# Expert token lists scattered to memory in the router, and experts run by falling count in three size classes

## The reference, cut to what matters

```
scores = sigmoid(x @ w_router)                      # (1088, 64)
biased = scores + router_bias
# 8 groups of 8 experts; the best 4 groups by the sum of their two best stay
_, idx = top_k(where(group_kept, biased, -inf), 8)  # 8 experts for each token
sel = take_along_axis(scores, idx, axis=1)
wts = sel / sum(sel) * 2.5
for e in range(64):
    tok = tokens with e in idx
    y[tok] += wts * ((silu(x[tok] @ w_gate[e]) * (x[tok] @ w_up[e])) @ w_down[e])
out = y + shared_expert(x)
```

## Time and profile before

| | |
|---|---|
| median of three runs | 2150.04 us (2149.35 to 2150.91) |
| span of the profiled execution | 2147.0 us |
| PE busy | 1883.8 us, 88% |
| PE weight loads busy | 1525.1 us, 71% |
| DVE busy | 1348.0 us, 63% |
| ACT busy | 868.2 us, 40% |
| POOL busy | 400.5 us, 19% |
| mean granted clock of TensorE | 0.928 |
| read from HBM, written | 330.71 MB, 66.34 MB |

### The profile page before, as it was taken

How to read it: one execution, slowest core, us unless ns; L and a number is a source line. 1 busy time by engine, 2 the same in 40 slices (tenths; PEclk the granted TensorE clock), 3 DMA queues, 4 the chain that set the end, 5 groups by cost and what they waited for, 6 DMA issues and landing times. The chain is left out here.

```text
span 2147.0 us, 35537 instructions
## 1 busy us (share of the span) xinstructions
PE 1883.8 (88%) x12638; PEld 1525.1 (71%) x12639; DVE 1348.0 (63%) x2002; ACT 868.2 (40%) x1392; POOL 400.5 (19%) x367
## 2 busy tenths in 40 slices
PE   7999999789968998899999989989989898747887
PEld 4566665457757897888888878888888798633433
DVE  3333433269856786767777777767666677556774
ACT  2122222133224555455555545555545555431111
POOL 0100001000011111211111121121111112135662
PEclk9999999889979998999999999999989899878999
DMA  9000000210066776767777777777676687655652
GB/s 358 35 0 0 0 0 13 85 52 29 30 208 221 255 267 219 258 225 252 263 251 246 258 244 248 251 258 264 227 254 235 226 277 247 214 203 179 229 199 103
DMA packets 104971, 396.27 MB, mean 185 GB/s; under 512 B 13230, under 2 KB 26990, under 8 KB 87901
## 3 DMA queue, kind: packets, MB, share of 16 engines
q1 hardware_dynamic: 61877, 245.27, 34.3%
q0 software_dynamic: 27264, 95.08, 13.0%
q10 hardware_dynamic: 15808, 55.65, 6.4%
HBM read 330.71 MB, written 66.34 MB: 185 GB/s over the span
## 5 line engine op out<-in xcount | busy, mean ns | idle before, releaser
L1352 POOL DMA_INDIRECT rows<-rows_dram,idx x132 | 228.2, 1728 | 1085.0 <-issue 1085.0
L1364 PE MATMUL GU<-x_hi,hi_g 128*128 128x212 f32 x1024 | 283.2, 277 | 0.0
L1364 PE MATMUL GU<-x_hi,hi_u 128*128 128x212 f32 x1024 | 282.7, 276 | 0.0
L1364 PE MATMUL GU<-x_lo,hi_g 128*128 128x212 f32 x1024 | 281.6, 275 | 0.0
L1364 PE MATMUL GU<-x_hi,lo_g 128*128 128x212 f32 x1024 | 281.2, 275 | 0.0
L1364 PE MATMUL GU<-x_lo,hi_u 128*128 128x212 f32 x1024 | 280.7, 274 | 0.0
L1364 PE MATMUL GU<-x_hi,lo_u 128*128 128x212 f32 x1024 | 280.3, 274 | 0.0
L1387 PE MATMUL T<-ident,rows 128*128 128x128 f32 (+1 forms) x1040 | 149.3, 314 | 137.9 <-DMA rows<-rows_dram,idx 137.9
L1522 DVE TENSOR_TENSOR x_lo<-T,x_hi 128x424 fp32r<-128x424 f32 x260 | 145.5, 595 | 144.8 <-ACT x_hi L1447 135.8
L1387 PEld LDWEIGHTS T<-ident,rows 128*128 128x128 f32 (+1 forms) x1040 | 132.9, 178 | 140.9 <-issue 140.9
L183 DVE TENSOR_TENSOR lo_u<-raw_u,hi_u 128x2048 fp32r<-128x2048 f32 x65 | 149.0, 2293 | 124.8 <-ACT hi_u L176 124.8
(11 more groups left out here) (240 smaller groups left out, 3481.0 us busy)
## 6 DMA issues: line engine op xcount, KB each, us to landing
raw_g<-in_w_exp_gate SPq DMA_DIRECT2D x65, 1024.0 KB, 7.0
raw_u<-in_w_exp_up SPq DMA_DIRECT2D x65, 1024.0 KB
raw_d<-in_w_exp_down SPq DMA_DIRECT2D x65, 1024.0 KB, 7.7
y_dram<-y ACTq DMA_DIRECT2D x64, 512.0 KB
y_dram<-y ACTq DMA_DIRECT2D x64, 336.0 KB
rows_dram<-row SPq DMA_DIRECT2D x9, 512.0 KB, 2.7
w_big<-in_w_in SPq DMA_DIRECT2D x2, 2048.0 KB, 12.4
w_out<-in_w_out SPq DMA_DIRECT2D x1, 4096.0 KB, 18.1
```

What stands on the lines that cost most here:

```text
L1352: pool.indirect_dma_start(out=rows[0:BLK[b], b, :], out_offset=None, in_=rows_dram[:, :], in_offset=bass.IndirectOffsetOnAxis(ap=idx[0:BLK ...
L1364: ins = pe.matmul(out, lhs[x], rhs[w], start=first and i == 0, stop=last and i == 2)
```

## The change

1. **Lists in memory.** `list_dram` holds for each place in a list and each expert a pair (token, row for an overflow). It is filled with a spare value in the mixer, by one transfer from a constant. In the router VectorE computes for each pair an `entry` = place x 64 + expert, and GpSimd scatters eight transfers of 128 values of 8 bytes for each tile (`enter`). After the last tile SP loads the first 256 places of all lists into `lists`.
2. **Ranks.** After the last tile two small matmuls and some ten VectorE operations rank the experts by count (expert 0 is always first, since its weights are loaded already), give `order`, and for each expert the first row of its results and its cap (`base_dram`).
3. **Three classes.** The expert stage runs the experts by rank: 16 with 212 rows, 16 with 164 (128 + 36), 32 with 128. Each class is a loop and, written out behind it, its last expert, which prepares one of the next class's size. All tiles of tokens, hidden layer and rows are cut to the class's size. Where an expert has more tokens than its cap, a general loop (`each_extra`) runs over all 64 experts with 128 rows; for none it does nothing.
4. **No list work in the expert stage.** `make_list`, `to_index` and `one_hot` are gone. GpSimd copies the index out of `lists` and gathers as soon as the transposes of the expert before are done. With each of the first nine experts GpSimd also gathers, in eight transfers of 8-byte values, the bases of one tile's pairs (`find_rows`); VectorE makes `slots` from them after the 16th expert.
5. The 65th expert is not prepared. Stores of the two blocks have a semaphore each.

```diff
...
-CAP = 212
-ROUNDS = -(-(SEQ + NS) // CAP)
-BLK = (P, CAP - P)
-OVER_ROW = E * CAP
-SPARE_ROW = OVER_ROW + (SEQ + NS) * TOP
-Y_ROWS = SPARE_ROW + CAP
+SIZES = ((212, 16), (164, 16), (128, 32))
+CAP = SIZES[0][0]
+RANK_CAP = [cap for cap, n in SIZES for _ in range(n)]
+RANK_ROW = [sum(RANK_CAP[:r]) for r in range(E)]
+TWO_BLOCKS = sum(n for cap, n in SIZES if cap > P)
...
+            sp.dma_start(list_dram[0:LIST_ROWS * E].rearrange("(p n) a -> p (n a)", p=LIST_ROWS), c["list0"]).then_inc(
+                keep["list_set"], 16)
...
+            sp.wait_ge(keep["listed"], 16 * TILES * TOP)
+            sp.dma_start(keep["lists"][:], list_dram[0:2 * P * E].rearrange("(b p e) a -> p b e a", b=2, e=E)).then_inc(
+                list_ld, 16)
+            sp.wait_ge(list_ld, 96)
+            sp.wait_ge(based, 1)
+            sp.dma_start(base_dram[:, :], base_i[:]).then_inc(base_st, 16)
+            sp.wait_ge(base_st, 16)
...
+            def enter(t):
+                pool_after(pool, keep["passed"], entry_ready, t + 1)
+                for k in range(TOP):
+                    pool.indirect_dma_start(
+                        out=list_dram[:, :], out_offset=bass.IndirectOffsetOnAxis(
+                            ap=entry[:, t, k:k + 1] if isinstance(t, int) else
+                            entry[:, bass.ds(t, 1), k:k + 1].rearrange("p a k -> p (a k)"), axis=0),
+                        in_=value[:, t, k, :], in_offset=None).then_inc(keep["listed"], 16)
...
+            norm(1)
+            pool.wait_ge(list_ld, 16 * 5)
+            pool.wait_ge(keep["list_set"], 16)
+            for t in range(TILES):
+                if t + 2 < TILES:
+                    norm(t + 2)
+                enter(t)
...
             def places(t):
                 dve.wait_ge(count_done, t + 1)
-                own.did(dve.scalar_tensor_tensor(out=pe_pos[:], in0=C[:, 0:E], scalar=1.0, in1=maskf[:],
-                                                 op0=ALU.add, op1=ALU.mult))
-                own.wait()
-                own.did(dve.tensor_copy(place[:, 0:E, t], pe_pos[:]))
+                own.did(dve.tensor_tensor(pe_pos[:], C[:, 0:E], maskf[:], ALU.mult))
                 own.did(dve.tensor_tensor(sofar[:], sofar[:], maskf[:], ALU.add))
+                own.wait()
+                dve.tensor_copy(sums[:, 0:1], sums[:, 1:2]).then_inc(placed, 1)
                 hot_sum(pe_pos[:], pos8[:, t, :])
-                own.wait()
-                dve.tensor_copy(sums[:, 0:1], sums[:, 1:2]).then_inc(placed, 1)
+                pos = pos8[:, t, :]
+                if isinstance(t, int) and t == LAST:
+                    own.did(dve.tensor_tensor(spared[:], pos, spare, ALU.add))
+                    own.wait()
+                    pos = spared[:]
+                own.did(dve.tensor_copy(keep["chosen"][:, bass.ds(t * TOP, TOP)], i8[:]))
+                dve.scalar_tensor_tensor(out=entry[:, t, :], in0=pos, scalar=float(E), in1=idx8[:, t, :],
+                                         op0=ALU.mult, op1=ALU.add).then_inc(entry_ready, 1)
...
+            own.did(dve.scalar_tensor_tensor(out=key[:], in0=C[0:E, 0:E], scalar=float(E), in1=tie[0:E, 0:E],
+                                             op0=ALU.mult, op1=ALU.add))
...
+            dve.tensor_scalar(at_rank[:], iota_e[0:E, :], rank[:], None, ALU.is_equal).then_inc(ranks_ready, 1)
...
+def each_job(eng, body, skip=0):
+    first = 0
+    for i, (cap, n) in enumerate(SIZES):
+        following = SIZES[i + 1][0] if i + 1 < len(SIZES) else None
+        with eng.Fori(max(first, skip), first + n - 1) as job:
+            body(job, cap, cap)
+        body(first + n - 1, cap, following)
+        first += n
+def each_extra(eng, keep, body):
+    n = eng.value_load(keep["extra"][0:1, 0:1], min_val=0, max_val=EXTRA)
+    with eng.Fori(0, n) as r:
+        with eng.Fori(0, E) as rank:
+            body(r, rank, E + r * E + rank)
+def blocks(cap):
+    return [(b, min(P, cap - b * P)) for b in range(-(-cap // P))]
...
+            sp.wait_ge(rows_ld[0], 16)
+            with sp.Fori(0, E - 1) as n:
+                e = sp.value_load(order[0:1, bass.ds(n + 1, 1)], min_val=0, max_val=E - 1)
+                at = sp.snap(n * GATE_PIECE)
+                load(e, n + 1)
...
+            def gather(tokens, cap):
+                for b, n in blocks(cap):
+                    pool.indirect_dma_start(
+                        out=rows[0:n, b, :], out_offset=None, in_=rows_dram[:, :],
+                        in_offset=bass.IndirectOffsetOnAxis(ap=tokens[0:n, b:b + 1], axis=0),
+                    ).then_inc(rows_ld[b], 16)
+            def fetch(job, cap):
+                e = pool.value_load(order[0:1, bass.ds(job, 1)], min_val=0, max_val=E - 1)
+                pool_after(pool, keep["passed"], x_tr, 4 * job + 1)
+                n = len(blocks(cap))
+                pool.tensor_copy(idx[:, 0:n], lists[:, 0:n, bass.ds(e, 1), 0].rearrange("p b e -> p (b e)")).then_inc(
+                    idx_ready, 1)
+                pool_after(pool, keep["passed"], idx_ready, job + 1)
+                gather(idx, cap)
+            fetch(0, CAP)
+            def find_rows(t):
+                for k in range(TOP):
+                    at = t * TOP + k
+                    pool.indirect_dma_start(
+                        out=keep["based"][:, at, :], out_offset=None, in_=base_dram[:, :],
+                        in_offset=bass.IndirectOffsetOnAxis(ap=keep["chosen"][:, at:at + 1], axis=0)).then_inc(base_ld, 16)
+            def job(n, cap, following):
+                if following:
+                    fetch(n + 1, following)
+            for n in range(TILES):
+                fetch(n + 1, CAP)
+                find_rows(n)
+            each_job(pool, job, TILES)
...
-            def make_list(j, h, rows_read):
-                pe.wait_ge(hot_ready, h + 1)
-                pe.wait_ge(idx_ready, j + 1)
-                pe.wait_ge(x_lo_ev, rows_read)
-                for b in range(2):
-                    for t in range(TILES):
-                        ins = pe.matmul(L[:, 2 * b:2 * b + 2], hot[:, t, b * P:(b + 1) * P], tok[:, t, :],
-                                        start=(t == 0), stop=(t == TILES - 1))
-                ins.then_inc(l_done, 1)
...
+            def transposes(m, cap):
+                pe.wait_ge(rows_ld[0], 16 * m + 16)
+                if cap > P:
+                    pe.wait_ge(rows_ld[1], 16 * m + 16)
...
+            def gate_up(m, cap):
+                pe.wait_ge(x_lo_ev, 4 * m + 5)
+                for mat, off in (("g", 0), ("u", cap)):
                     pe.wait_ge(lo_set[mat], m + 1)
                     for f in range(FC):
                         for k in range(KC):
                             w = slice(f * P, (f + 1) * P)
-                            ins = three(GU[f][:, off:off + CAP], (hi[mat][:, k, w], lo[mat][:, k, w]),
-                                        (x_hi[:, k, :], x_lo[:, k, :]), k == 0, k == KC - 1)
+                            ins = three(GU[f][:, off:off + cap], (hi[mat][:, k, w], lo[mat][:, k, w]),
+                                        (x_hi[:, k, 0:cap], x_lo[:, k, 0:cap]), k == 0, k == KC - 1)
...
+            def job(n, cap, following):
+                gate_up(n, cap)
+                if following:
+                    transposes(n + 1, following)
+                down(n, cap)
+            each_job(pe, job)
...
+            def job(n, cap, following):
+                rank = RANK_CAP.index(cap)
+                first = (n - rank) * cap + RANK_ROW[rank]
+                first = first if isinstance(n, int) else act.snap(first)
+                act.activation(warm[:], warm[:], ACT.Sigmoid).then_inc(warmed, 1)
+                if following:
+                    act.wait_ge(ld["g"], 16 * n + 32)
+                    act.wait_ge(g_used, n + 1)
+                    split_hi(act, keep, "g", n + 1, 0)
+                sigmoids(n, cap)
+                if following:
+                    x_parts(n + 1, following)
+                    act.wait_ge(ld["u"], 16 * n + 32)
+                    split_hi(act, keep, "u", n + 1, 0)
+                for b, rows_b in blocks(cap):
+                    if not (isinstance(n, int) and n == 0):
+                        act.wait_ge(y_st[b], 16 * n + 1)
+                    copy_out(n, cap, b, rows_b, 0)
+                    if b == 0 and following:
+                        split_hi(act, keep, "u", n + 1, 1)
+                    copy_out(n, cap, b, rows_b, 1)
+                    store(first, n, b, rows_b)
+                if following:
+                    act.wait_ge(ld["d"], 16 * n + 32)
+                    split_hi(act, keep, "d", n + 1, 0)
...
+            def rows_of_tokens():
+                row, is_over, shift = (slot_f[:, i, :] for i in range(3))
+                dve.wait_ge(base_ld, 16 * TILES * TOP)
+                own.did(dve.tensor_tensor(row, keep["based"][:, :, 0], keep["pos8"][:], ALU.add))
...
+            def job(n, cap, following):
```

(82 more changed lines are left out.)

460 lines of the change are left out of this document (166 added, 294 removed).

## The result

The changed kernel takes 5213.0 us at the median of four runs (5208.6 to 5228.1), the kernel before 2149.7 (2145.8 to 2150.9). The ratio is 2.426, 95% interval 2.421 to 2.431. The forecast was 1903, faster.

A forecast was written before the change was run, and what follows sets the result against it. TensorE was taken as the bound, losing 205.8 us to late gathers and half clock. Terms -258.7 (stage), +3.6 (router), +13 and +2 (handover), -6.8 (end) sum to -246.9: span 1900.1, run 1903; range 1870 to 1975.

The forecast's parts named there:

- An overflow pass, slower than before: Rival, expert stage: one expert over its cap sends all 64 through the general loop, at least 1366 us, 3270; 2%.
- my bound: General loop in an overflow: at least 64 x (14.45 + 6.9 for the splits) us, weights not loaded ahead.
- Down matmuls stay as they are: Expert stage: down matmuls unchanged by the size classes, since one-block experts skipped the second block already.
- In the 164 class they shrink to 36 columns, 0.3: Expert stage: second-block transposes in the 164-row class narrow, saving 0.3 us an expert, giving 17.5.
- My price of a transpose: Expert stage: a transpose of 84 columns costs 0.073 us, from the 1.48 us that 16 take.
- the first step: Expert stage: earlier gathers remove the 34 waits and the half clock behind them; gain 205.8 us, less 2.2.
- 2 for the clock: Router to first expert: 2 us more for a clock that has been low for longer.
- Columns count: Rival, expert stage: gate-up matmuls with fewer columns take less time, 103 us more gain, 1800; 5%.
- GpSimd is the bound: Rival: GpSimd limits router (9 x 2) and first experts (9 x 3.5) where it got work; +50, 1953; 17%.
- The weight chain: Rival, last class: weight loading at 265 GB/s bounds an expert at 16.1 us; +52, 1955; 17%.
- 3.6 + 13: Delay of the first gate-up: router +3.6 us for VectorE's entries, handover to the first expert +13.

The follow-up runs named there:

- e1_guard: Changed kernel with the loop over overflow passes put in If(n > 0) on all engines: 2115.4 us, ratio 0.980 to the kernel before.
- e2_guard_ahead: e1_guard with semaphore y_ev starting at 2, as in the kernel before, not 1, and two waits moved by 1: 1962.9 us, ratio 0.913.
- e11_in_pairs: e2_guard_ahead with each expert's 16 transposes reordered, two of 128 partitions then two of 36, instead of one and one: 1923.9 us, ratio 0.897.
- e12_in_eights: e11_in_pairs with all eight transposes of 128 partitions first, then the eight of 36: 1914.7 us, ratio 0.893.
- e4_two_classes: e2_guard_ahead without the 164-row class, 32 experts of 212 rows and 32 of 128: 1908.1 us, ratio 0.888.
- e8_base_first: e4_two_classes with SyncE storing the experts' first rows ahead of its wait for the scatters: 1905.8 us, ratio 0.886.

## Why the prediction was wrong, point by point

**The step that failed in kind: "An overflow pass, slower than before".** The mechanism was among the rivals with 2%, but I let it hang on the 33rd count and argued that nothing overflows. Nothing does. I never asked what the loop does when its count is 0; `Fori` with an end held in a register does not skip. The kernel before has the same loop over rounds, where the count is at least 1, so no row of it could show this. It costs 3064 us in the changed kernel's profile (the output stage starts at 4993 instead of 1924.2 + 4.6). Its size was off as well: at least 21.35 us an expert by my bound, 48 measured, as scatter, list, gather and transposes stand in one chain and TensorE falls to half clock. With 2% on it, 5213 lay outside the range, and beyond that rival's own 3270.

**"Down matmuls stay as they are".** They don't: the deletion of one `sem_inc` makes each half wait for the one before. e1_guard to e2_guard_ahead: 152.5 us by the medians, 156.2 by the two profiled executions. These 156.2 are 43 in the first class (20.68 against 17.80 an expert), 86 in the middle one, whose clock gains too, and (15.57 - 14.62) x 32 = 30 in the last, less 3.4 by which the first gate-up is later. How much of the 86 is waits and how much clock is not told apart. I compared waits line by line but not the starting values of the semaphores; the deleted line is in the change.

**"In the 164 class they shrink to 36 columns, 0.3".** The sign was wrong: transposes of 36 rows between ones of 128 cost 2.0 us more an expert, and clock behind that. Worth 54.8 us. My price of a transpose was a mean by columns from the earlier trace rows, where 84 partitions stand beside 128. The kernel before does have 64 beside 128, in the mixer's matmuls at L540 and L542 (shown with e11_in_pairs and e12_in_eights): there a change cost 0.067, and the clock fell from 1.00 to 0.50 at 411, behind sixteen such pairs; whether they let it fall no run tests. That was the place to find this term.

**What was right, measured with these three mended (e4_two_classes).** Spacing 17.80 and 14.62 (forecast 17.8 and 14.45); 0.5 us of waits for gathered rows in all, clock 1.00, so the 205.8 us of the first step are there. The stage takes 1041.4 (628.10 to 1669.54), forecast 1028.7 and 2 for the clock: of the 11 between them 5 are the second sixteen experts at 17.8 and not 17.5, 5 the last class at 14.62. 95 gaps of 128-column gate-up matmuls take 10.56 us, 0.111 each as at 212 columns, so *Columns count* falls, and the weight load stays the likely pace. The 81 ns of the Trainium skill's "TensorE: Matmul & The Clock Gate", "Back-to-back issue gap", aren't reached here. The first gate-up is at 627.3 to 631.1 in the runs with the guard (626.6 in e8_base_first), against 614.7; the forecast was 3.6 + 13 later, 631.3. From the end of the last down matmul (1669.54) to the output stage (1674.16) it takes 4.6, forecast 5.5. *GpSimd is the bound* falls: the nine experts with extra gathers are at 17.8 to 18.3. *The weight chain* falls: 280 GB/s in the last class with TensorE busy 466.89 of 467.80 us. The three faults account for the whole. 54.8 (the transposes) and 152.5 (the lost count) lead from 1908.1 to 2115.4 by themselves, since they are differences of these times; the pass is checked on its own: 2115.4, 3064 from the profile and the 38 of half clock in the middle class are 5217, against 5213 measured. That 1908.1 lies so near 1903 is in part luck: the 11 that the stage takes more stand beside errors the other way, such as the first gate-up, 3 sooner than forecast.

## What to carry to other kernels

For each loop whose end is a runtime value, ask what it does at 0, and put an `If` around it unless the value is known to be positive; a fallback path that "never runs" is best counted in the trace, by its DMA issues. When a change touches a hand-written semaphore protocol, compare starting values and increments as well as waits: a lost start of 1 takes away the double buffering and shows only in the time. Before adding a size class, ask whether it puts matmuls of 64 partitions or fewer between wider ones; pad them above 64 or group them. And look for such a pattern in every stage of the trace at hand: another stage may already show its price. Last, try the one-line edit that the diagnosis names first: here it had 59% of the gain.

## What the runs showed of the hardware

A change between transposes on 128 partitions and on at most 64 costs TensorE about 0.134 us a time (3.47, 2.40, 1.59 us for 16, 8, 2 changes), with a step between 72 and 64 partitions (1.38 and 3.63 us for 16 transposes). Between matmuls of 128 and 64 partitions with 32 stationary and 64 moving columns it costs 0.067 (0.146 to 0.149 against 0.080, mixer of the kernel before), so it is the partitions read, not the columns. Without such a change transposes of 36 partitions come 0.062 apart, those of 128 come 0.109 apart (e12_in_eights). The granted clock fell to 1.2 GHz (0.50) behind transposes that change sixteen times, though TensorE's busy time in that stretch is 303.00 of 303.00 us; the ends of matmuls are modelled, so a short pause at each change would not show in it. In e12_in_eights the same transposes, grouped, left the clock at 1.00. A hardware loop whose end is a register that holds 0 ran its body once: its one comparison came behind the body on all five engines.
